# Half tiles of 64 columns kept only in the loop of the experts' up projection; whole tiles in its last two chunks and in the gather

## The reference

```python
def moe_ffn(u, w_router, w13, w2):
    t = u.reshape(-1, D)
    logits = (t @ w_router).astype(jnp.float32)
    top_val, top_idx = lax.top_k(logits, TOP_K)
    top_w = jax.nn.softmax(top_val, axis=-1)
    out = jnp.zeros_like(t)
    for e in range(N_EXPERTS):
        gate_e = jnp.sum(jnp.where(top_idx == e, top_w, 0.0), axis=-1).astype(t.dtype)
        out = out + gate_e[:, None] * swiglu(t, w13[e], w2[e])
    return out.reshape(Bsz, S, D)
```

## Time and profile before

| | |
|---|---|
| median of 3 runs | 3860.64 us (3860.27 to 3860.99) |
| the profiled execution, own time | 3851.47 us |
| its span, first to last instruction | 3849.6 us |
| mean granted TensorE clock | 0.921 |
| busy: matmul / weight load / VectorE / ScalarE | 86% / 72% / 30% / 11% |
| the eight experts in the span | from 2867.7 to about 3818 us |

### The profile page before, as it was taken

One profiled execution on the slowest core, in us unless ns is written; L12 is line 12 of the kernel. 1 busy time (PEld: TensorE's weight loads), 2 busy tenths in 40 slices (PEclk: granted clock), 3 DMA queues, 4 the chain that ended last, 5 costly groups with the idle time before them and its releaser, 6 DMA issues.

```text
span 3849.6 us, 56613 instructions
## 1 busy us (share of the span) xinstructions
PE 3309.0 (86%) x24234; PEld 2782.2 (72%) x24235; DVE 1154.9 (30%) x2082; ACT 425.1 (11%) x944; POOL 140.3 (4%) x77
## 2 busy tenths in 40 slices
PE   5999998899999999899997789931379988899887
PEld 4888887788888888788887578821266775567764
DVE  6204222320412312241133434379731111111112
ACT  0000112000000012010002000011111111111111
POOL 0000000000000000000000000045300000000000
PEclk9999999899999998999997799965679999999999
DMA  8636433363653742355362057500028766687764
GB/s 310 235 152 235 177 142 110 131 238 150 221 208 137 260 142 99 110 214 199 128 255 92 14 193 283 207 36 0 22 75 352 302 273 258 271 342 312 277 262 179
DMA packets 51292, 731.71 MB, mean 190 GB/s; under 512 B 6112, under 2 KB 6296, under 8 KB 9620
## 3 DMA queue, kind: packets, MB, share of 16 engines
q1 hardware_dynamic: 47636, 716.70, 49.3%
q0 software_dynamic: 3456, 12.00, 0.9%
HBM read 727.59 MB, written 4.23 MB: 190 GB/s over the span
## 4 chain that ended last, share of the span: by engine, by line
PE 78%; DVE 12%; DMA 5%; issue 4%; ACT 1%; DVEq 0%; POOL 0%; SPq 0%; POOLq 0%
PE psum L528 59%; PE psum L914 8%; PE psum L598 2%; DVE ada_sum L1181 2%; DMA ring<-in_down_e_dram 2%; DMA ring<-in_up_dram 1%; PE psum L728 1%; PE psum L892 1%; PE psum L554 1%; DVE work L1718 1%; DVE work L1719 1%; PE psum L928 1%; DVE work L1706 1%; DVE work L1707 1%; PE psum L567 1%
## 5 line engine op out<-in xcount | busy, mean ns | idle before, releaser
L528 PE MATMUL psum<-h_t,ring 128*64 128x96 f32 (+1 forms) x17600 | 1883.6, 297 | 58.7 <-DVE h_t L1263 25.1
L528 PEld LDWEIGHTS psum<-h_t,ring 128*64 128x64 f32 (+1 forms) x17600 | 1686.6, 158 | 239.0 <-issue 62.6
L528 PE MATMUL psum<-work,ring 128*128 128x256 f32 x2752 | 610.4, 385 | 28.2 <-ACT work L1063 10.6
L528 PEld LDWEIGHTS psum<-work,ring 128*128 128x128 f32 x2752 | 531.6, 194 | 106.1 <-issue 14.3
L1219 DVE TENSOR_TENSOR work<-work,psum 128x256 f32 (+1 forms) x302 | 127.3, 421 | 1034.7 <-PE psum L528 955.6
L1181 DVE SCALAR_TENSOR_TENSOR ada_sum<-ring,cond,ada_sum 128x512 f32<-128x512 f32 x420 | 315.8, 752 | 18.2 <-DVE ada_sum L1181 3.6
L914 PE MATMUL psum<-ring,work 128*96 128x512 f32 x704 | 303.8, 593 | 8.7 <-DMA ring<-in_down_e_dram 7.3
L914 PEld LDWEIGHTS psum<-ring,work 128*96 128x96 f32 x704 | 114.1, 163 | 193.1 <-issue 193.1
L978 ACT ACTIVATE work<-psum 128x256 f32<-128x256 f32 x302 | 115.5, 383 | 1155.3 <-PE psum L528 1155.1
L1230 DVE SCALAR_TENSOR_TENSOR x_t<-psum,mod,x_t 128x256 f32<-128x256 f32 x64 | 31.0, 484 | 455.7 <-PE psum L528 455.7
L892 PE MATMUL psum<-work 128*64 128x96 f32 x512 | 40.3, 351 | 80.9 <-issue 77.0
(11 more groups left out here) (289 smaller groups left out, 1760.3 us busy)
## 6 DMA issues: line engine op xcount, KB each, us to landing
ring<-in_up_e_dram SPq DMA_DIRECT2D x88, 2048.0 KB, 9.2
ring<-in_ada_dram SPq DMA_DIRECT2D x60, 2048.0 KB, 7.9
ring<-in_up_dram SPq DMA_DIRECT2D x55, 2048.0 KB, 7.9
ring<-in_down_e_dram SPq DMA_DIRECT2D x32, 2816.0 KB, 12.4
ring<-in_down_dram SPq DMA_DIRECT2D x20, 2816.0 KB, 9.3
ring<-in_w_qk_dram SPq DMA_DIRECT2D x12, 2048.0 KB, 7.9
ring<-in_w_ccch_dram SPq DMA_DIRECT2D x8, 2048.0 KB, 7.8
ring<-in_w_gates_dram SPq DMA_DIRECT2D x8, 2048.0 KB, 7.9
```

The source lines that it names most:

```text
L528: mm = pe.matmul(half(b)[lo:hi, 0:width], w[:, lo:hi], moving(k, j * lin.groups + m), start=(k == 0), stop=(k == depth - 1))
```

## The change

The test which cuts the columns is given a different width at two places. In `linear` it gets the real width only where `i` is a register, that is, in the hardware loop; in straight code it gets 256, and so makes whole tiles. In the gather it always gets 256. How many columns move (`0:width`) stays as it was, 96 in the short branch.

```diff
--- before.py
+++ after.py
@@ -524,7 +524,7 @@
                             w = ring[:, slot, (m * depth + k) * P:(m * depth + k + 1) * P]
-                            for lo, hi in columns_of(width):
+                            for lo, hi in columns_of(S if isinstance(i, int) else width):
                                 mm = pe.matmul(half(b)[lo:hi, 0:width], w[:, lo:hi], moving(k, j * lin.groups + m),
                                                start=(k == 0), stop=(k == depth - 1))
@@ -888,7 +888,7 @@
                     for t in range(TT):
-                        for lo, hi in columns_of(width):
+                        for lo, hi in columns_of(S):
                             mm = pe.matmul(half(b)[lo:hi, 0:width], h_tok[:, t, f * P + lo:f * P + hi],
                                            sel[:, t, 0:width], start=(t == 0), stop=(t == TT - 1))
```

## The result

The changed kernel takes 3895.34 us (median of 4 runs, 3891.59 to 3897.11) against 3860.45 us before (4 runs, 3855.22 to 3860.99): ratio 1.0092, 95% interval 1.0075 to 1.0110. It is slower, by 34.9 us between the medians. The profiled execution took 3893.99 us with a span of 3892.1 us, 42.5 us more than the span before; the profiled execution of the kernel before had been 9.2 us under its median, this one is 1.4 us under its own. The clock granted was 0.915 in the mean, against 0.921.

The account below looks back on a forecast made before the run. It took TensorE, busy 86% of the span, to bound the kernel. +27.7 us for the up chunks, +7.1 for the gather and 0 for the gap gave +34.8, so 3895 us against the median; own range 3885 to 3904, wider range 3855 to 3904.

Parts of the forecast that it names:

- the sum: Over the experts: +27.7 for the up chunks, +7.1 for the gather, 0 for the gap, together +34.8 us.
- The rate of whole tiles: TensorE's products with 128 weight columns and 96 moving ones: 113 ns each at full clock, range 84 to 113.
- The rate of the halves: Half tiles in the up projection: 41.5 ns a record, 83 ns for the two replacing one whole tile.
- Rival 3: Up chunks and gather: a whole tile is no dearer than its halves, only some 4 us lost, 3865 us; chance 0.04.
- Part 1: Last two up chunks of each expert: +30.8 us for 8 experts, 3.1 us absorbed by existing waits, so +27.7 us.
- Part 2: The gather: whole tiles at partly low clock, +5.9 us for 7 experts and +1.2 for the first, +7.1 us.
- 4.4 + 1.4 = 5.8 us: Each gather behind a gap: 20 records at 215 ns in low clock, then 12 at 113 ns.
- Part 3: The gap ahead of L892: TensorE's waiting for code, 77.0 us in 7, unchanged, with about 9 blocks a round.
- Rival 1: Gaps ahead of L892: all code of a round fits, up to 77.0 us vanish, 3818 us; chance 0.09.
- Rival 2: Gaps ahead of L892: only the loop's head stays stored, 35 us back, 3860 us; chance 0.11.

Follow-up runs that it names:

- e1_tail_only: The kernel before with whole tiles in the last two up chunks alone, half tiles kept in the gather: 3889.89 us.
- the repeated pair: The kernel before and the changed kernel, both unchanged, run and profiled again on one chip: 3856.68 us and 3899.67 us.
- the kernel moved by 75: e7_four_rounds with its experts' loop moved on by 75 instructions, through waits placed far ahead of the experts: 3792.33 us.
- e4_after_no_long: The changed kernel without TensorE's long branch, which these inputs never take: 3805.79 us.
- e2_gather_only: The kernel before with whole tiles in the gather alone: 3874.74 us.
- e7_four_rounds: The four-round kernel: against the kernel before, all up chunks in one four-round loop, third chunk skipped in the last round, whole tiles in the gather: 3781.19 us.
- e3_whole_all: The changed kernel with whole tiles everywhere, so also in the up projection's loop: 3943.48 us.
- e8_four_rounds_half: e7_four_rounds with half tiles kept in the gather, 64 instructions more: 3855.54 us.
- e9_half_shifted: e8_four_rounds_half with its experts' loop moved on by 160 instructions, through waits placed far ahead of the experts: 3782.76 us.

## Why the prediction was right

The forecast was 3895 us, the measurement 3895.34. The mechanism holds, but that the two meet within 1 us is luck: the experts take 40.4 us longer where the sum had 34.8, and it is the scatter of the runs that put the medians 34.9 apart. So the steps one by one.

**The rate of whole tiles.** Taken as 113 ns from rows with 64 and with 128 moving columns; measured 113.6. The rate of the halves was taken as 41.5 and is 41.8 over all. The rule from the Trainium skill ("TensorE: Matmul & The Clock Gate", section "LDWEIGHTS (loading the stationary operand)") is near for the whole tile (107) and not for the half (53 against 41.8 measured). Rival 3, which it led to, is out.

**Part 1.** +30.8 us forecast and measured, 3.1 absorbed forecast and 3.0 measured, with the down projection waiting 0.71 us in every expert. `e1_tail_only` gives +27.0 for it alone, against 27.7.

**Part 2.** Undersized: +7.1 us forecast, +9.7 measured and +14.1 for the gather's edit alone, its waits for up chunks among them. The term that failed is the length of the seven gathers behind a gap, "4.4 + 1.4 = 5.8 us"; they measured 5.59 to 6.85, 6.1 in the mean, and the first 7.30 where 6.9 was forecast. The term took the clock's rise at the same 4.4 us from the gather's start. The stretches of the changed kernel (length, busy, granted clock, DMA share, GB/s) show a second and a third gather that differ in just this:

```profile
2998.00:3003.60 5.60, 5.58 (x32) 0.66 0.00 0
3121.70:3128.50 6.80, 6.80 (x32) 0.53 0.00 0
```

At a clock of 0.66 the gather takes 5.60 us, near the forecast 5.8; at 0.53 it runs at the low level nearly to its end. Why the clock rises earlier in one gather than in the next, no run shows. A whole tile loses more in the low clock (215 ns against 113) than a pair of halves (about 160 against 83; one half takes (2.83 - 0.35) / 31 = 80 ns in the first gather of the earlier trace rows, less the last one's own 0.35 us), so the work that stands behind a gap is the worst place for it.

**The costs left out.** The waits for up chunks, +2.9 us in one profile and +2.7 in the other, had no term. They and the gather make the stretch of the experts 40.4 and 38.3 us longer, not 34.8. The medians first measured are 34.9 apart, those of the repeated pair 43.0.

**Part 3.** Unchanged gap forecast, 77.6 us measured, with the 9 blocks a round that the text worked out. The reason was right too: it is the wait for code, and the four-round kernel, with one block fewer by its packets, has lost it. The rule of the Trainium skill ("Runtime: NRT & Kernel Launch", section "Instruction fetch mechanics"), a store of 2048 instructions in eight blocks, oldest out first, had only been cited; the runs here agree with it, but for the kernel moved by 75: 8 blocks stay, 9 are all fetched again. Rival 1 is real, but as a property of another kernel; its price of 77 us was what dropping the gap gave back, and more, since the gather then runs at full clock: 92.4 us on the stretch of the experts from the change to `e4_after_no_long`, 86.1 from `e2_gather_only` to `e7_four_rounds`. Rival 2, only the head survives, is what the second expert of `e3_whole_all` shows for one round; it cannot last with a store that gives up the oldest.

## What to carry to other kernels

Count the instruction packets of one round of an outer loop before trimming its code: as long as the count is above what the engine keeps, each instruction saved takes nothing off the wait, and where the count falls to what is kept the whole wait goes at once. A branch that is only jumped over costs blocks at its far side, and the place of the code against the block borders can be worth as much as its length, so remove straight copies of loop bodies first, since without them the engine was no slower (the up projection takes 58.4 us in `e7_four_rounds`, 58.65 before). When tiles are priced, take the time from start to start in rows of the same weight shape, on both sides of the missing size, and at the clock that the place really has.

## What was not expected of the hardware

Moving code by 160 instructions, with nothing else changed, took 73 us from 3856 (`e8_four_rounds_half` and `e9_half_shifted`). A fetch in the gap costs far more than its transfer: where one jump misses its block TensorE stands still for 5.7 to 6.8 us, against 0.7 where it finds it, while a packet of 16 KB takes some 1 to 2 us (an estimate from the two packets of `e3_whole_all`, 1.9% of 16 engines in 7 us, and the two of the earlier trace rows, 6.7% in 3.5 us). And the half tiles' advantage is not the same at both clocks in what it saves: 64 halves take 2.86 us at full clock and 4.1 to 5.4 behind a gap, 32 whole ones 3.78 and 5.5 to 7.1.
